# Value drains moved to ScalarE, scores issued early, two weight splits moved to VectorE, the last head reordered, and GpSimd's weight splits cut into four instructions

## The reference, cut to what matters

```python
proj = rms_norm(h, g_mix) @ w_in              # q, k, v, xr, gr: 512 columns each
o = diff_attention(rope(q), rope(k), v, lam)  # 4 heads: softmax(s0) - lam * softmax(s1), times v
o = rms_norm(o, g_subln) * (1 - lam_init)
y = rg_lru(conv(xr)) * gelu(gr)               # a linear recurrence over the tokens
h = h + concat([o, y]) @ w_out
h = h + square(relu(rms_norm(h, g_mlp) @ w_mlp_in)) @ w_mlp_out
h = h + sigmoid(rms_norm(h, g_ple) @ w_ple_gate) * (p @ w_ple_proj)
```

## Time and profile before

| | us |
|---|---|
| median of 3 runs | 2648.98 (2646.34 to 2650.09) |
| the profiled execution, its own time | 2649.76 |
| its span, first to last instruction | 2648.0 |
| PE busy | 2436.3 (92%) |
| DVE busy | 1516.7 (57%) |
| ACT busy | 835.7 (32%) |
| POOL busy | 350.3 (13%) |

### The profile page before, as it was taken

How to read it: one execution, slowest core, us unless ns; L and a number is a source line. 1 busy time by engine, 2 the same in 40 slices (tenths; PEclk the granted TensorE clock), 3 DMA queues, 4 the chain that set the end, 5 groups by cost and what they waited for, 6 DMA issues and landing times. The chain is left out here.

```text
span 2648.0 us, 29239 instructions
## 1 busy us (share of the span) xinstructions
PE 2436.3 (92%) x11390; PEld 1955.5 (74%) x11398; DVE 1516.7 (57%) x2122; ACT 835.7 (32%) x1155; POOL 350.3 (13%) x219
## 2 busy tenths in 40 slices
PE   7988999998998899999888897999979889899996
PEld 5866888887786688888765676888856567688885
DVE  6774544455687445445478856444447984744544
ACT  4454222233435322223232343222223234322221
POOL 1011000000201100001024512000022541200002
PEclk9999999999999999999889998999989999899998
DMA  4211222221221132222121211222212111122222
GB/s 146 104 49 58 92 91 99 105 96 67 92 88 64 48 112 96 95 95 96 48 88 50 78 37 60 100 101 100 89 55 89 64 64 48 62 98 96 95 95 79
DMA packets 33301, 217.75 MB, mean 82 GB/s; under 512 B 4128, under 2 KB 4384, under 8 KB 7840
## 3 DMA queue, kind: packets, MB, share of 16 engines
q1 hardware_dynamic: 33184, 216.18, 23.1%
HBM read 214.07 MB, written 2.10 MB: 82 GB/s over the span
## 5 line engine op out<-in xcount | busy, mean ns | idle before, releaser
L323 PE MATMUL ps<-gh,wh 128*128 128x512 f32 (+1 forms) x1728 | 699.3, 405 | 109.3 <-DVE gl L464 65.4
L323 PE MATMUL ps<-gl,wh 128*128 128x512 f32 (+1 forms) x1728 | 681.9, 395 | 0.0
L323 PE MATMUL ps<-gh,wl 128*128 128x512 f32 (+1 forms) x1728 | 681.6, 394 | 0.0
L307 ACT ACTIVATE wh<-wr 128x2048 fp32r<-128x2048 f32 x196 | 374.0, 1908 | 560.2 <-PE ps L323 560.0
L313 DVE TENSOR_TENSOR wl<-wr,wh 128x2048 fp32r<-128x2048 f32 x172 | 394.8, 2295 | 248.9 <-ACT wh L307 248.9
L323 PE MATMUL ps<-hh,wh 128*128 128x512 f32 x1280 | 504.7, 394 | 7.4 <-DVE hl L944 3.1
L323 PE MATMUL ps<-hh,wl 128*128 128x512 f32 x1280 | 499.8, 390 | 0.0
L323 PE MATMUL ps<-hl,wh 128*128 128x512 f32 x1280 | 499.3, 390 | 0.0
L323 PEld LDWEIGHTS ps<-gh,wh 128*128 128x128 f32 (+1 forms) x1728 | 328.7, 190 | 211.0 <-DVE gl L464 72.7
L323 PEld LDWEIGHTS ps<-gl,wh 128*128 128x128 f32 (+1 forms) x1728 | 328.4, 190 | 72.8 <-issue 5.3
L323 PEld LDWEIGHTS ps<-gh,wl 128*128 128x128 f32 (+1 forms) x1728 | 328.0, 190 | 72.0
(11 more groups left out here) (204 smaller groups left out, 2414.4 us busy)
## 6 DMA issues: line engine op xcount, KB each, us to landing
wr<-in_weights SPq DMA_DIRECT2D x198, 1024.0 KB, 4.7
x<-in_xt SPq DMA_DIRECT2D x1, 2048.0 KB, 11.8
out_yt<-x SPq DMA_DIRECT2D x1, 2048.0 KB, 7.2
tmp<-in_positions SPq DMA_DIRECT2D x4, 256.0 KB, 3.3
arena<-in_gates SPq DMA_DIRECT2D x2, 512.0 KB, 4.8
arena<-in_embed SPq DMA_DIRECT2D x2, 512.0 KB, 5.6
par<-in_params_b SPq DMA_DIRECT2D x2, 274.0 KB, 3.1
par<-in_params_a SPq DMA_DIRECT2D x2, 157.5 KB, 2.7
```

What stands on the lines that cost most here:

```text
L307: act.activation(mem.wh[:, c % 2, :], mem.wr[:, c % 2, :], ACT.Copy).then_inc(sem["high"], 1)
L323: done = pe.matmul(out, stationary, moving, start=(first and n == 0), stop=(last and n == 2), skip_group_check=True)
```

## The change

Eight edits. In each layer of the first stack: (1) ACT drains the eight value tiles (`keep_values`), and these tiles alternate between banks 0 and 1, so that PE waits for the tile before the last. (2) PE issues scores 0 and 1 after the fifth and sixth value tile; ACT does exponents 0 and 1 between the last value drains. (3) The recurrence's product alternates between two slots of `tmp`, and its subtraction (`y_low`) is put one `recur` later. (4) The low parts of A_Y and A_Y + 1 are DVE's: the first between `maxima(0)` and `maxima(1)`, the second in step 2. (5) After the last step PE puts the last head's back transpose before the third head's products, and both splits of chunk A_O + 1 go ahead of the last head's rounding and subtraction. (6) In the additions to x, DVE does `gain_low` of slice k - 1 after the addition of slice k; ACT rounds chunk A_MLP after slice 1 and DVE subtracts it after the addition of slice 3. In each layer of the second stack: (7) POOL's ten low parts are made by four instructions of 128x512 instead of one of 128x2048 (`split_low_in_parts`). (8) `token_tile` has a number of banks as an argument; the second stack keeps four.

```diff
+def split_low_in_parts(pool, mem, sem, c):
+    pool.wait_ge(sem["high"], split_count(c))
+    for at in range(0, CHUNK, S):
+        part = slice(at, at + S)
+        last = pool.tensor_tensor(mem.wl[:, c % 2, part], mem.wr[:, c % 2, part], mem.wh[:, c % 2, part].bitcast(F32), ALU.subtract)
+    last.then_inc(sem["low"], 1)
...
-    pe.wait_ge(sem["drained"], tile - 3)
+    pe.wait_ge(sem["drained"], tile + 1 - banks)
...
 # POOL, first stack
-                pool.wait_ge(sem["low"], split_count(A_Y - 1))
-                split_low(pool, mem, sem, A_Y)
-                split_low(pool, mem, sem, A_Y + 1)
...
 # ACT, first stack
+                def keep_values(n):
+                    tile, c, i = A_TILE[A_V] + n, n // QT, n % QT
+                    act.wait_ge(sem["product"], tile + 1)
+                    act.wait_ge(sem["drained"], tile)
+                    act.activation(v[:, i, c * CW:(c + 1) * CW], ps[:, a_bank(tile), 0:CW], ACT.Copy,
+                                   scale=small[:, QT + i:QT + i + 1]).then_inc(sem["drained"], 1)
...
+                y_high(0)
+                keep_values(0)
+                keep_values(1)
+                y_high(1)
+                keep_values(2)
+                y_high(2)
+                keep_values(3)
+                y_high(3)
+                split_high(act, mem, sem, A_Y, a_used(A_Y))
+                keep_values(4)
                 exponents(0)
+                keep_values(5)
+                exponents(1)
+                keep_values(6)
+                keep_values(7)
                 for s in range(STEPS):
-                    if s + 1 < STEPS:
+                    if 0 < s < STEPS - 1:
                         exponents(s + 1)
...
+                split_high(act, mem, sem, A_O + 1, a_used(A_O + 1))
                 output_high(HEADS1 - 1)
-                split_high(act, mem, sem, A_O + 1, a_used(A_O + 1))
...
-                    if c == A_O:
-                        split_high(act, mem, sem, A_MLP, a_used(A_MLP))
+                        if c == A_O and t == 1:
+                            split_high(act, mem, sem, A_MLP, a_used(A_MLP))
...
 # DVE, first stack
+                recur(0)
+                split_low(dve, mem, sem, A_V + 1)
+                for t in range(1, 4):
+                    recur(t)
+                    y_low(t - 1)
+                y_low(3)
                 maxima(0)
+                split_low(dve, mem, sem, A_Y)
                 maxima(1)
                 for s in range(STEPS):
                     mix(s)
                     if s + 2 < STEPS:
                         maxima(s + 2)
+                    if s == 2:
+                        split_low(dve, mem, sem, A_Y + 1)
...
+                split_low(dve, mem, sem, A_O + 1)
                 output_low(HEADS1 - 1)
-                split_low(dve, mem, sem, A_O + 1)
...
+                for k in range(KT):
+                    add_to_x(A_TILE[A_O] + k, k)
+                    if k:
+                        gain_low(dve, mem, sem, 1, k - 1, mlp_gains)
+                    if k == 3:
                         split_low(dve, mem, sem, A_MLP)
+                gain_low(dve, mem, sem, 1, KT - 1, mlp_gains)
...
 # PE, first stack
+                for c in (A_V, A_V + 1):
+                    for i in range(QT):
+                        token_tile(pe, mem, sem, c, i, A_TILE[c] + i, 2)
+                        if c > A_V and i < 2:
+                            scores(i)
                 pe.wait_ge(sem["drained"], A_TILE[A_Y])
-                scores(0)
-                scores(1)
...
                     pe.wait_ge(sem["o_low"], k + 1)
+                    if k == 2:
+                        turn_back(HEADS1 - 1, STEPS)
                     for t in range(4):
                         half_tile(A_O, t, (k,), False)
-                turn_back(HEADS1 - 1, STEPS)
...
 # POOL, second stack: ten calls a layer
-                split_low(pool, mem, sem, 4)
+                split_low_in_parts(pool, mem, sem, 4)
```

More of the change, by code:

```diff
@@ L372, in first_two_chunks, with token_tile @@
             spread_root(pe, mem, sem, n)
-def token_tile(pe, mem, sem, c, i, tile):
+def token_tile(pe, mem, sem, c, i, tile, banks=4):
     if i == 0:
         pe.wait_ge(sem["low"], split_count(c))
-    pe.wait_ge(sem["drained"], tile - 3)
+    pe.wait_ge(sem["drained"], tile + 1 - banks)
     wh = mem.wh[:, c % 2, :].rearrange("p (k n) -> p k n", k=KT)
@@ L382, in token_tile @@
     for k in range(KT):
-        last = three_passes(pe, mem.ps[:, tile % 4, 0:CW], wh[:, k, :], wl[:, k, :],
+        last = three_passes(pe, mem.ps[:, tile % banks, 0:CW], wh[:, k, :], wl[:, k, :],
                             mem.gh[:, k, i * P:(i + 1) * P], mem.gl[:, k, i * P:(i + 1) * P], k == 0, k == KT - 1, swap=True)
@@ L513, in a_bank @@
 def a_bank(tile):
-    return tile % 2 if A_TILE[A_Y] <= tile < A_TILE[A_O] else tile % 4
+    return tile % 2 if A_TILE[A_V] <= tile < A_TILE[A_O] else tile % 4
 SM_C8, SM_NC8, SM_X, SM_E, SM_S, SM_S2, SM_PL, SM_LAM, SM_GS = 16, 20, 24, 28, 32, 36, 40, 44, 50
@@ L649, in _, with y_high @@
                 split_high(act, mem, sem, 9, a_used(9))
-                for t in range(4):
+                def y_high(t):
                     act.wait_ge(sem["y_ready"], t + 1)
-                    act.activation(mem.hh[:, 4 + t, :], tmp[:, 1, :], ACT.Copy).then_inc(sem["y_high"], 1)
-                split_high(act, mem, sem, A_Y, a_used(A_Y))
+                    act.activation(mem.hh[:, 4 + t, :], tmp[:, t % 2, :], ACT.Copy).then_inc(sem["y_high"], 1)
+                def keep_values(n):
[4 more added lines that the diff above has]
+                                   scale=small[:, QT + i:QT + i + 1]).then_inc(sem["drained"], 1)
                 def exponents(s):
@@ L875, in recur, with y_low @@
                     dve.wait_ge(sem["gelued"], t + 1)
[L876 removed]
+                    if t >= 2:
+                        dve.wait_ge(sem["y_low"], t - 1)
+                    dve.tensor_tensor(tmp[:, t % 2, :], ii[:, t, :], gr[:, t, :], ALU.mult).then_inc(sem["y_ready"], 1)
+                def y_low(t):
                     dve.wait_ge(sem["y_high"], t + 1)
[L878 removed]
+                    dve.tensor_tensor(mem.hl[:, 4 + t, :], tmp[:, t % 2, :], mem.hh[:, 4 + t, :].bitcast(F32),
                                       ALU.subtract).then_inc(sem["y_low"], 1)
@@ L887, in _ @@
                             gain(t)
[L888 to L902, removed]
                 def maxima(s):
@@ L962, in _ @@
                     if s in (6, 10):
-                        if s == 6:
-                            dve.wait_ge(sem["low"], split_count(A_Y + 1))
                         split_low(dve, mem, sem, A_PROJ + s // 4 - 1)
@@ L974, in _ @@
                 output_norm(HEADS1 - 1)
+                split_low(dve, mem, sem, A_O + 1)
                 output_low(HEADS1 - 1)
-                split_low(dve, mem, sem, A_O + 1)
[L978 to L981, removed]
-                            dve.wait_ge(sem["drained"], A_TILE[A_O])
-                        add_to_x(A_TILE[c] + t, k)
-                        gain_low(dve, mem, sem, 1, k, mlp_gains)
-                    if c == A_O:
+                dve.wait_ge(sem["drained"], A_TILE[A_O])
+                for k in range(KT):
[3 more added lines that the diff above has]
+                    if k == 3:
                         split_low(dve, mem, sem, A_MLP)
+                gain_low(dve, mem, sem, 1, KT - 1, mlp_gains)
                 split_low(dve, mem, sem, A_MLP + 1)
@@ L1069, in _ @@
                     linear_chunk(c, mem.gh, mem.gl)
-                for c in (A_V, A_V + 1):
-                    for i in range(QT):
-                        token_tile(pe, mem, sem, c, i, A_TILE[c] + i)
                 def scores(s):
```

8 lines of the change are left out of this document (4 added, 4 removed).

## The result

| | us | ratio to before, 95% interval |
|---|---|---|
| before, 4 runs | 2648.82 (2646.34 to 2650.09) | |
| after, 4 runs | 2607.11 (2603.61 to 2607.97) | 0.9843 [0.9831, 0.9856] |
| predicted | 2602 (2590 to 2620) | |

The change takes 41.7 us off. The spans of the two profiled executions, 2648.0 and 2606.2, differ by 41.8, so the traces can be subtracted. PE is busy for 2427.2 us (93%) where it was 2436.3: the same matmuls, 9 us less of half speed. The other 33 us are idle time of PE.

The account below looks back on a forecast made before the run. PE, busy 92%, was held by idle stretches and slow clock, with DVE stalled behind POOL's long instructions and full in the second stack. First stack 33 plus second 14 made 47 us off 2649.8, median 2602, range 2590 to 2620.

Parts of the forecast that it names:

- the forecast (both stacks gain): Whole kernel: first and second stack both get faster, 2590 to 2612 us, chance 0.60.
- start of attention and steps: First stack, per layer: 7.35 us saved up to step 1's transpose, less 0.4 for a split on DVE.
- last head, MLP start, clock: First stack, per layer: PE's waits there go, 6.15 us, and the half-clock stretch behind them returns 3.4.
- masks off the path: Second stack, per layer: PE's 3.89 us wait for DVE's masks gives way to ACT's last value drain, 3.4 gained.
- PE's own path, picking: Second stack's picking stage, per layer: the chain to POOL's low part starts sooner, 2.4 us gained, bounds 0 and 3.5.
- Waits of 0.85, 0.5 and 0.5: First-stack value tiles and first step: new waits for drains of the first, fifth and last tile, in us.
- The 0.4 for DVE's second split: First stack, step 2: A_Y + 1's split on DVE costs about 0.4 us a layer, bounds 0 and 2.3.
- Rival B (the slow clock stays): Both stacks: new short waits keep the half-clock stretches at 1.2 GHz, 2615 us, chance 0.17.
- Rival A (POOL does not let DVE in): Second stack: the four parts hold DVE as one, so nothing is gained there, 2619 us, chance 0.17.
- Rival C: POOL's small instructions are dear: each part has a fixed cost of 1.02 us, slower at 2677 us, chance 0.02.
- Net 2.4: Second stack's picking stage, per layer: chain 2 to 3 us sooner, three splits 0.5 longer each, rotary additions' other waits gone.
- Attention stage, 1.2: Second stack, attention behind picking, per layer: the clock's fall and a similar stall give 1.2 us, bounds 0 and 3.

Follow-up runs that it names:

- experiment 2: Kernel before with only the last head reordered, additions ahead of subtractions and the MLP chunk rounded earlier (edits 5 and 6): 2628.10 us, 0.9922.
- Experiments 3 and 4: Third: kernel before with only the low parts of A_Y and A_Y + 1 moved to DVE, 2644.92 us. Fourth: kernel after without early scores and exponents, 2622.44 us.
- experiment 1: Kernel after with POOL's second-stack splits whole again, 2614.49 us; with two parts of 128x1024 a split instead of four, 2607.25 us.
- Experiment 5: Kernel after with 24 unneeded matmuls ahead of chunk 7 and 14 ahead of the last pooling product in each second-stack layer: 2600.85 us, 0.9819.
- Experiment 6: Kernel after with chunk 7's split ahead of POOL's first rotary addition, 2600.93 us; with POOL's whole second-stack order rewritten, 2592.79 us.
- experiment 4: Kernel after without early scores and exponents, 2622.44 us; the same with 15 unread matmuls filling PE's first-stack waits, 2615.08 us.
- experiment 7: Kernel after with POOL's second-stack order rewritten, plus its five splits whole, 2606.36 us; or plus 8 and 16 filling matmuls, splits in parts, 2594.16 us.

## Why the prediction was right, and where its terms were off

The time, 2607, lies in the range of the forecast (both stacks gain), 5 us from its centre. The cause was the one named: DVE instructions standing behind POOL's long ones, and an order that left PE waiting. By its terms, two layers each:

| term | predicted | measured | from |
|---|---|---|---|
| start of attention and steps | 2 x (7.35 - 0.4) = 13.9 | 14.6 | 34.9 - 20.3; in layer 1 the last step ends 7.3 sooner |
| last head, MLP start, clock | 2 x (6.15 + 3.4) = 19.1 | 20.3 | experiment 2 |
| first stack | 33.0 | 34.9 | the first picking stage, 1421.31 and 1386.46 |
| masks off the path | 2 x 3.4 = 6.8 | 6.6 | wait of 3.89 to 0.56, twice |
| PE's own path, picking | 2 x 2.4 = 4.8 | 0.2 | -0.1 in layer 1 (77.53 and 77.60 us), 0.3 in layer 2 (77.57 and 77.31) |
| attention stage and what follows | 2 x 1.2 = 2.4 | 0.1 | attention -0.6 and -0.5 (88.01 us after, 87.43 before in layer 1), the rest 0.1 and 1.1 |
| sum | 47 | 41.8 | spans |

**Start of attention.** Waits of 0.85, 0.5 and 0.5 were foreseen; 0.60, none and 0.56 came. The right size hides how it comes about. I added up matmuls and waits and laid the gain to the missing stalls and to the order alike. Experiments 3 and 4 show that it isn't a sum: edit 4 alone gives 1.7 a layer (0.4 to 2.9), edits 1, 3 and 4 without 2 nothing that can be told, all together 7.3. In both experiments waits were left in front of the steps, and the half clock behind them ate what the others saved. The 0.4 for DVE's second split was right: the steps from the second on take 66.06 us for 65.60.

**Last head and clock.** Right in every wait but 0.37. That the clock would follow the waits was an assumption with bounds of 0 and 3.4; experiment 2 shows it. Rival B (the slow clock stays) fell for the first stack.

**POOL's parts.** Rival A (POOL does not let DVE in) is refuted by L1577's longest of 1.7 us and by experiment 1: whole splits cost 7.4 us. Rival C fell with 1.355 a part; its fixed cost, with 1.355 and 4.62 for a quarter and the whole, is 0.27 a part, not 1.02, and a part of it is the turns below.

**The term that failed: "Net 2.4".** By its own parts (2 to 3 sooner, 1.5 for three longer splits, 0.6 for each of the three waits ahead of the last product) it comes to 2.4 to 3.4, so the value was the low end, and it was still too high. Its first half held: the first rotary addition starts 2.97 us sooner (1398.17, and before 1435.99, less the 34.85 by which the stage began later) and PE's wait for the low part is 6.36, foreseen as near 6.5. DVE's own stage got shorter by 8.6 us up to the end of the masks, just under the 9 to 13 foreseen (11.8 up to their start, but the three of them then took 4.09 us beside POOL's parts for 0.90). The waits of the other rotary additions went as well (36.2 in 10 became 23.6 in 2). The second half did not: POOL, which now never waits from 1398 to 1450, is the bound of the stage, and its work got longer by more than I had charged. POOL's timeline, kernel after:

```profile
1399.39 5.40 POOL L322 TENSOR_TENSOR wl<-wr,wh 128x512 fp32r<-128x512 f32 x4
...
1426.20 1.73 POOL L1326 TENSOR_TENSOR arena<-arena,tmp 128x512 f32<-128x512 f32 x1
```

A split takes 5.0 to 5.5, not 5.1, and rotary additions up to 1.76, not 1.28, where DVE works beside them. From the split of chunk 7 to the last pooling product it is 43.5 us for 41.7, although three waits of 0.63 in it went: POOL's work there grew by 3.7 us, where I had charged 1.5. PE's waits for its products grew by 0.25 and 0.36, and the clock fell during more of PE's work. In numbers: the last pooling product comes 1.2 us sooner in each layer, counted from the stage's start (56.45 us for 57.63 and 57.65), and of this the value tiles behind it, at half clock for longer, give back 1.3 in layer 1 and 0.9 in layer 2. Experiment 5 sizes all of the half clock that is left on the path at 2.6 and 2.1. Experiment 6 shows that the bound was POOL's order: split 7 alone moved gives 6.2 us, the whole order 14.3.

**Attention stage, 1.2.** I had it from the clock's fall behind the wait for the masks. That wait went, but the stage still holds a stretch at half clock of the same length (1476.3 to 1479.7, before 1503.7 to 1507.1), now behind a wait of 1.86 inside its own steps that was there before as well (1.97). That it moved makes the 0.6 us that the stage takes longer. It left the first scores, where it cost 1.0 (from PE's third scores to the next row that waits it was 5.15 us and is 4.16), and lies behind that wait in the steps, where it costs 1.6 (13.59 us from there to the next such row, 12.03 before). All the other stretches between these rows agree within 0.1.

The Trainium skill (GPSIMD Engine Reference, Specifications) says that GpSimd shares its SBUF interfaces with VectorE, and that VectorE's instructions with two SBUF inputs contend, as do those in a 2-port mode. The trace agrees: L1577, with two inputs in SBUF, takes 2.27 us in the mean in the kernel with whole splits and 1.17 in the one with parts, while its neighbour L1575, with one input in PSUM, takes 0.67 in both.

## What to carry to other kernels

A wait on the matmul engine costs more than its length where the clock falls behind it: price a stage's waits together, since removing only some of them gave nothing here (experiment 4). When a shared engine's long instruction is cut so that others get in, ask which of the two is then the bound: it pays for the turns. Here reordering POOL's queue gave 14.3 us on top of the cutting and 8.1 with the stage's splits whole in both orders (2614.5 and 2606.4), and the cutting gave 7.4 in the old order and 13.6 in the new one: each is worth more with the other. Filling matmuls are a cheap test of how much of a stage is clock: they gave 6.3 us where PE waited for POOL, and left the stage at 71.37 us where DVE was the bound. But look where the gain falls, since some 3 of the 6.3 us lay in a later stage, and see that the filling ends before what PE waits for is there.

## What the runs showed of the hardware

POOL and DVE take turns by instruction, and both are stretched. DVE's 128x512 multiplication with two SBUF inputs (0.68 us alone) had a median of 1.29 among POOL's parts, at most 1.68. POOL's 128x512 addition (1.28) took up to 1.76. Three mask instructions of DVE took 4.09 us beside POOL's parts (kernel after, 1455.09) and 0.90 where POOL was idle (experiment 7).

The clock fell behind short waits as behind long ones. In experiment 4 it was 0.50 from 147.20 on, after PE had waited 1.20, 0.56 and 0.71 us (up to 138.00, 144.58 and 146.85). Fifteen matmuls of some 0.23 us each (16 in 3.81 us, experiment 7) in the waits of that stretch kept it at 1.00:

```profile
117.50:160.00 42.50, 41.20 (x284) 35.00 (x284) 29.70 (x50) 18.16 (x39) 0.00 (x0) 1.00 0.16 63
```
